# Latent attention's scores and values: the 16 meta keys as products of their own, and a new table of places for VectorE and ScalarE

## The reference

```python
s = (jnp.einsum('bqhd,bkhd->bhqk', qn, k_nope, preferred_element_type=jnp.float32)
     + jnp.einsum('bqhr,bkr->bhqk', qr, k_rope, preferred_element_type=jnp.float32)) * scale
q_idx = blk * Q_BLOCK + jnp.arange(Q_BLOCK)
mask = (key_idx[None, :] <= q_idx[:, None]) & (key_idx[None, :] >= pad)
s = jnp.where(mask[None, None], s, MASK_VALUE)
p = jax.nn.softmax(s, axis=-1)
return jnp.einsum('bhqk,bkhd->bqhd', p.astype(v.dtype), v)
```

## Time and profile before

| | |
|---|---|
| median of 3 runs | 844.8 us (844.73 to 845.4) |
| the profiled execution's own time | 846.0 us |
| span of its instructions | 844.2 us |
| PE busy | 818.6 us, 97% |
| DVE busy | 560.8 us, 66% |
| ACT busy | 532.3 us, 63% |
| granted TensorE clock, mean | 0.995 |

### The profile page before, as it was taken

One profiled execution on the slowest core, in us unless ns is written; L12 is line 12 of the kernel. 1 busy time (PEld: TensorE's weight loads), 2 busy tenths in 40 slices (PEclk: granted clock), 3 DMA queues, 4 the chain that ended last, 5 costly groups with the idle time before them and its releaser, 6 DMA issues.

```text
span 844.2 us, 16068 instructions
## 1 busy us (share of the span) xinstructions
PE 818.6 (97%) x6612; PEld 786.2 (93%) x6612; DVE 560.8 (66%) x1004; ACT 532.3 (63%) x962; POOL 2.6 (0%) x6
## 2 busy tenths in 40 slices
PE   6999999999999998899999999999999999999994
PEld 6997769999999898899999999999899999999994
DVE  6685658889988976567536553876758656465353
ACT  6478766589977868763544545668867546444442
POOL 0000000000000000000000000000000000000001
PEclk9999999999999999999999999999999999999998
DMA  8453215555745432445645764444336737374431
GB/s 313 150 188 113 63 51 172 191 162 210 231 170 170 124 124 98 155 171 166 221 163 181 250 193 150 150 151 144 107 108 217 242 119 253 113 258 167 148 101 50
DMA packets 41448, 137.39 MB, mean 163 GB/s; under 512 B 4384, under 2 KB 8736, under 8 KB 41376
## 3 DMA queue, kind: packets, MB, share of 16 engines
q1 hardware_dynamic: 41376, 136.37, 49.0%
HBM read 135.31 MB, written 1.05 MB: 162 GB/s over the span
## 4 chain that ended last, share of the span: by engine, by line
PE 94%; DVE 3%; ACT 1%; DMA 1%; issue 0%; DVEq 0%; ACTq 0%; SPq 0%
PE bank L666 26%; PE bank L668 26%; PE bank L667 25%; PE bank L671 2%; PE bank L939 2%; PE bank L672 2%; PE bank L673 2%; PE bank L891 1%; PE bank L892 1%; DVE temp L1449 1%; PE bank L860 1%; DVE residual L1449 1%; PE bank L919 1%; DMA weights_raw<-stream_dram 1%; PE bank L920 1%; DVE weights_lo L1449 1%
## 5 line engine op out<-in xcount | busy, mean ns | idle before, releaser
L666 PE MATMUL bank<-operand_hi,weights_hi 128*128 128x256 f32 (+1 forms) x1860 | 529.5, 285 | 10.9 <-DVE weights_lo L1449 7.8
L668 PE MATMUL bank<-operand_hi,weights_lo 128*128 128x256 f32 (+1 forms) x1860 | 526.7, 283 | 0.0
L667 PE MATMUL bank<-operand_lo,weights_hi 128*128 128x256 f32 (+1 forms) x1860 | 526.6, 283 | 0.0
L666 PEld LDWEIGHTS bank<-operand_hi,weights_hi 128*128 128x128 f32 x1860 | 352.4, 189 | 16.3 <-DVE weights_lo L1449 8.7
L668 PEld LDWEIGHTS bank<-operand_hi,weights_lo 128*128 128x128 f32 x1860 | 352.8, 190 | 0.0
L667 PEld LDWEIGHTS bank<-operand_lo,weights_hi 128*128 128x128 f32 x1860 | 350.8, 189 | 0.0
L1016 ACT ACTIVATE weights_hi<-weights_raw 128x1024 fp32r<-128x1024 f32 (+2 forms) x254 | 258.3, 1041 | 130.1 <-PE bank L668 92.5
L1449 DVE TENSOR_TENSOR weights_lo<-weights_raw,weights_hi 128x1024 fp32r<-128x1024 f32 (+2 forms) x254 | 298.5, 1205 | 52.5 <-ACT weights_hi L1016 52.4
L1449 DVE TENSOR_TENSOR operand_lo<-temp,operand_hi 128x512 fp32r<-128x512 f32 (+2 forms) x48 | 28.4, 601 | 55.0 <-ACT operand_hi L1016 55.0
L1455 DVE SCALAR_TENSOR_TENSOR temp<-bank,rows 128x512 f32<-128x512 f32 x32 | 21.9, 688 | 40.6 <-PE bank L668 39.7
L671 PE MATMUL bank<-weights_hi,operand_hi 128*128 128x256 f32 (+1 forms) x140 | 41.6, 297 | 0.0
(11 more groups left out here) (177 smaller groups left out, 645.3 us busy)
## 6 DMA issues: line engine op xcount, KB each, us to landing
weights_raw<-stream_dram SPq DMA_DIRECT2D x244, 512.0 KB, 4.4
weights_raw<-stream_dram SPq DMA_DIRECT2D x6, 384.0 KB, 3.5
temp<-memT_dram SPq DMA_DIRECT2D x8, 256.0 KB, 3.4
residual<-xT_dram SPq DMA_DIRECT2D x4, 272.0 KB, 4.9
weights_raw<-stream_dram SPq DMA_DIRECT2D x4, 256.0 KB, 5.1
out_dram<-residual SPq DMA_DIRECT2D x3, 256.0 KB, 2.2
constants<-consts_dram SPq DMA_DIRECT2D x1, 536.0 KB, 7.8
out_dram<-residual SPq DMA_DIRECT2D x2, 128.0 KB, 2.1
```

What stands on the lines that cost most here:

```text
L666: e.matmul(to, w_h, x_h, start=start, stop=False, skip_group_check=True)
L667: e.matmul(to, w_h, x_l, start=False, stop=False, skip_group_check=True)
L668: return e.matmul(to, w_l, x_h, start=False, stop=stop, skip_group_check=True)
```

## The change

The scores' tiles of 144 and 272 keys become a product over the keys from the 17th on (128 or 256 columns) and one over the first 16 keys, for nope and for rope. The product of the meta values' 272 columns becomes one of 256 and one of 16. The columns, and what is added to them, are the same. `start` is set only on the first product of the first two tiles. The table `TIMES` is replaced as a whole; PE's places are not.

```diff
-    ("scalar", "lambda_exp"): (25.5,),
-    ("scalar", "mla_softmax"): (23.67, 24.57, 24.86, 25.23, 25.27, 25.58, 25.69, 25.81),
+    ("scalar", "lambda_exp"): (6.25,),
+    ("scalar", "mla_softmax"): (22.88, 26.27, 26.36, 26.64, 28.67, 29.2, 29.3, 29.55),
...
                 for j, (q0, nq, nk) in enumerate(TILES_A):
-                    to = bank[b][0:nq, PROB_AT[j]:PROB_AT[j] + nk]
-                    e.matmul(to, qn[:, h, q0:q0 + nq], kn[:, h, 0:nk], start=True, stop=False, skip_group_check=True)
-                    mm = e.matmul(to, qr[half:half + ROPE, pair_, q0:q0 + nq], kr[half:half + ROPE, 0, 0:nk],
-                                  start=False, stop=True, skip_group_check=True)
+
+                    keys = [(META, nk), (0, META)] if j else [(0, META)]
+                    for qt, kt, last in ((qn[:, h, :], kn[:, h, :], False),
+                                         (qr[half:half + ROPE, pair_, :], kr[half:half + ROPE, 0, :], True)):
+                        for k0, k1 in keys:
+                            mm = e.matmul(bank[b][0:nq, PROB_AT[j] + k0:PROB_AT[j] + k1], qt[:, q0:q0 + nq], kt[:, k0:k1],
+                                          start=j < 2 and not last and k1 == keys[0][1], stop=last, skip_group_check=True)
...
-                e.matmul(o[:, 0:T1], V16[0:META, cs], pt[0:META, 0:T1], start=True, stop=False, skip_group_check=True)
+                for t0, t1 in ((META, T1), (0, META)):
+                    e.matmul(o[:, t0:t1], V16[0:META, cs], pt[0:META, t0:t1], start=t0 > 0, stop=False,
+                             skip_group_check=True)
```

More of the change, by code:

```diff
@@ L165 @@
[L165 to L179, removed]
@@ L195 @@
[L195 to L208, removed]
@@ L209 @@
[L209 to L223, removed]
@@ L224 @@
-    ("vector", "evacuate"): (7.56, 7.89, 7.33, 7.44, 10.4, 12.43, 10.8, 12.57, 12.29, 12.71, 13.33, 18.5, 22.67,
[7 rows of a table removed]
-    ("vector", "finish"): (7.67, 9.33, 0, 10.1, 28.8, 28.2, 29.33, 30.2, 30.6, 32.25, 32.5, 32.88, 68.5, 68.75,
[4 rows of a table removed]
+    ("scalar", "root"): (6.75, 13.2, 11.75, 34.2, 36.5, 75.25, 101.5, 164.67, 192.25),
+    ("scalar", "row"): (8.5, 13.4, 13.8, 34.6, 36.75, 76.38, 75.5, 102.5, 165.5, 192.5),
+    ("scalar", "latent_hi"): (13.6, 15.67, 16.67, 16.33, 18.5),
+    ("scalar", "small"): (6.5,),
@@ new lines @@
+    ("scalar", "inputs_root"): (55.5, 55.25, 60.5, 60.75),
+    ("scalar", "silu_gates"): (58.5, 61.67),
+    ("scalar", "y_b"): (60.88, 60.12, 61.33, 60.62, 64.2, 64.4, 64.6, 64.8),
+    ("scalar", "softmax"): (76.12, 76.25, 76.62, 77.33, 80.18, 80.09, 80.55, 80.45, 86.4, 86.2, 86.8, 87.33, 90.42,
+        90.75, 90.83, 90.5, 166.5, 166.75, 167.5, 168.22, 172.58, 172.08, 172.83, 172.67, 178.17, 178.33, 178.5,
+        178.58, 183.23, 183.15, 183.62, 183.46),
+    ("scalar", "softmax_scale"): (76.5, 76.75, 77.67, 77.83, 168.11, 168.33, 168.56, 168.89, 172.75, 172.5, 172.92,
+        173.33, 178.42, 178.67, 178.75, 178.83, 183.38, 183.54, 183.92, 183.77),
@@ new lines @@
+    ("scalar", "evacuate"): (9.33, 11.25, 11.5, 9.67, 10.5, 26.82, 19.5, 21.67, 15.33, 22.62, 22.12, 17.5, 20.33,
[7 rows of a table added]
+    ("vector", "total"): (0, 0, 0, 30.83, 0, 70.67, 98.67, 162.5, 189.9),
+    ("vector", "rstd"): (5.67, 12.2, 11.5, 32.2, 35.5, 72.5, 98.83, 162.75, 191.5),
+    ("vector", "rope_rows_a"): (8.38,),
+    ("vector", "latent_norm"): (12.8, 13.5, 14.38, 14.5, 17.33),
+    ("vector", "latent_rest"): (14.25, 14.75, 14.88, 17.67, 19.33),
+    ("vector", "small"): (4.5, 5.33, 17.83, 22.67, 25.5, 8.5),
@@ new lines @@
+    ("vector", "conv_rest"): (42.33, 41.4, 39.67, 42.67, 48.57, 48.43, 48.86, 48.93),
+    ("vector", "inputs"): (48.21, 48.71, 55.57, 57.25),
+    ("vector", "inputs_square"): (50.6, 50.2, 60.11, 60.39),
+    ("vector", "inputs_mult"): (55.71, 55.29, 60.56, 60.67),
+    ("vector", "scan"): (57.75, 55.86, 60.17, 55.43, 60.78, 60.89, 60.94, 61.4),
+    ("vector", "y_b"): (60.22, 57.5, 60.33, 60.44, 61.2, 61.6, 61.8, 62.33),
+    ("vector", "y_b_rest"): (60.72, 60.06, 60.83, 60.61, 62.17, 62.5, 62.67, 62.83),
@@ new lines @@
+    ("vector", "y_2"): (77.88, 79.75, 171.1, 173.4, 175.33, 178.75, 180.12, 180.62, 184.5, 186.5),
+    ("vector", "scale_x"): (77.38,),
+    ("vector", "merge"): (77.62, 79.25, 85.4, 85.8, 90.67, 90.83),
+    ("vector", "sub_mean"): (89.14, 92.33),
+    ("vector", "sub_norm"): (89.43, 92.67),
+    ("vector", "sub_turn"): (90.33, 90.5, 93.5),
+    ("vector", "evacuate"): (6.5, 6.25, 8.25, 6.75, 14.62, 8.88, 12.4, 12.6, 14.12, 17.17, 17.5, 19.67, 21.33,
[6 rows of a table added]
+    ("vector", "finish"): (8.12, 8.62, 0, 8.75, 30.5, 30.08, 30.33, 30.58, 30.75, 32.4, 32.8, 33.67, 69.4, 68.5,
[4 rows of a table added]
```

38 lines of the change are left out of this document (25 added, 13 removed), and 35 rows, old and new, of the table TIMES.

## The result

The changed kernel takes 850.3 us (848.92 to 852.23, 6 runs) against 845.3 us (844.73 to 845.76, 6 runs) before: a ratio of 1.006 with a 95% interval of 1.0046 to 1.0074, 5.0 us slower. Executions more than 1.5% above the fastest of their kernel are left out of every ratio here. A second set of runs of the same kernel, made beside the later experiments, gave 848.4 against 845.2 us: 1.0043 (1.0026 to 1.006), 3.2 us slower. The forecast was 848.8 us and slower, 847.3 to 850.3.

What follows compares the result with a forecast made beforehand. The prediction took PE's own work to bound the latent attention heads. 40 splits add +4.0 us and the table 0, so the median of 844.8 becomes 848.8 us, range 847.3 to 850.3.

Steps and rivals of the forecast that it cites:

- What bounds the kernel: Latent attention heads, 67.5 to 124 us: PE's own work sets the time; DVE and ACT have room.
- The price of a short product: 16-column products with 128-wide weights: two weight loads set 0.22 us each, about +0.10 us a split.
- The upper bound of +12 us: Split products: the long one keeps its wait, the short one shows its first load, +0.30 us a split.
- the lower of +0.9: Split products: a short one costs only 0.14 us, as with 16 wide weights, +0.02 us a split.
- about +8 us: Split products by the skill page's rule: same-row neighbours hide neither load, some 0.2 us a split.
- A change of rows, not the columns beyond 128s: Fp32 products in the heads: a changed contraction row count costs about 0.1 us behind a long product, whatever its columns.
- the rival: Heads' products: columns beyond whole 128s keep the next load waiting, so the split saves 3.0 us, 841.8; chance 0.11.
- The sum: Whole kernel: +4.0 us on PE's path from 40 splits, table 0, giving 848.8 us.
- The table: New `TIMES`: taken as 0, with -1 to +2 us, since PE's waits are the lengths of their chains.
- the -1 that I allowed: New `TIMES`: at most 1 us gained by taking away PE's waits.

Runs made afterwards that it cites:

- The double dose: The split with the table of before, each 16-column product cut again into two of 8 columns: 884.4 us, ratio 1.0453 against the kernel before.
- the order without a split: Kernel before with its table, the scores' three nope products in a row, then the three rope products: 842.5 us, ratio 0.9966.
- the split in the good order: Kernel before with its table, nope then rope products grouped, 16-column pieces split off in scores and values: 849.4 us, ratio 1.0054.
- the best one: Kernel before with grouped nope and rope products, the values' 16-row product moved last, and the new table: 839.2 us, ratio 0.9937.

## Why the prediction was right, point by point

**What bounds the kernel: right.** PE's own work set the time in the heads. What it got there (+4.1 us) moved everything behind it, and neither DVE nor ACT became late.

**The price of a short product: right.** 0.22 us was taken, from the row of the one-column products and from L983. The double dose gave 0.22 us for each added product at full clock. The upper bound of +12 us and the lower of +0.9 are out. By the sentence of the Trainium skill in "TensorE: Matmul & The Clock Gate", section "The mechanism", that a load overlaps matmuls in flight only when the row group differs, products over the same rows would hide no load, which the prediction put at about +8 us; the heads here gave +4.1. The same section also lets a load into the background weight buffer run ahead, which the prediction left out.

**A change of rows, not the columns beyond 128s: right against the rival, too narrow as a rule.** This was the step with a rival against it. Whole 128s took nothing off: with no change on either side, 144 columns take 0.247 us (the order without a split) and 128 columns 0.223 (the split in the good order), which is the price of the 16 columns and no more. But it isn't rows alone. The prediction's rule has L921 at 0.32 us because 16 rows follow; in front of scores it takes 0.32 us as well, with 128 rows and 16-wide weights behind it. The prediction had not read that row. And its 0.1 us "behind a long product" is half of the price: L920's 0.53 us, which it took as free of any change, had the 16-row product ahead of it. A product pays some 0.1 us when the change is behind it, and some 0.1 us when it is ahead. The forecast didn't suffer, since the split leaves every change where it was and only the short product takes it over.

**The sum: right for the split.** +4.0 us was taken, the heads cost 4.1 in the trace, and the split alone measured +4.4 us.

**The table: mis-sized.** I took 0, "such a wait is the length of its chain, and no order shortens it". The table alone gives -0.9 us, which is inside the -1 that I allowed. What I missed was no wait at all: I read PE's waits for what the table could take away, while 0.84 us lay in two heads' products running one behind the other with PE busy throughout, because ACT gave a bank back late. It shows in the distance from start to start of eight equal matmuls (1.98 us at 562 us, 1.14 at 558 us), which I had read for the latent attention only.

**The clock: not in the prediction.** The sum 845.3 + 4.4 - 0.9 = 848.8 is the forecast to the tenth, and the second set came out at 848.4. Some of that is luck: the forecast started 0.5 us too low, took 0.4 us too little for the split and 0.9 too much for the table, and these cancel. The first set came out at 850.3, with executions whose mean clocks, 0.988 to 0.994, all lay below the 0.995 and 0.996 of five of the other six. The prediction had the clock as the same before and after. Of all 18 executions of the split in the order of before, with either table, 7 have a mean clock of 0.993 or less, and of the kernel before 8 of 60. That leans towards the split bringing such stretches on, but 4 of the 7 come from one set, so it isn't shown. For the twice cut products (5 of 5), the good order with the split (8 of 9) and the good order alone with the table of before (9 of 12) it is plain that they come more often.

## What to carry to other kernels

Read what a product costs from the distance to the next start, and compare neighbours before columns: an odd size next to a change of contraction rows, or of the weights' width, looks dear though only the neighbour is. Order the products so that those over the same rows and with weights of the same width follow each other; that gave 0.49 us a head at full clock, where cutting off 16 columns added 0.42. A product with wide weights has a least price, 0.22 us here, whatever it moves. And look at the clock of the new order too. A list of waits shows only idle time; two pieces of work that could run side by side on PE and don't are found by comparing equal groups of instructions.

## What the hardware did that I had not expected

- **Two fp32 products on separate halves of the rows run side by side.** Eight matmuls of 256 columns, four for each of two heads with operands on 64 rows each, took 1.14 us when both heads' banks were free, and 1.98 us when the second bank came late. The latent attention's rope products use 64 rows, but each follows a nope product over all 128, so nothing there shows it.
- **A busy PE can lose its clock.** In the kernel with the short products cut once more, PE was busy for 30.40 of 30.40 us between 119.6 and 150 us at a granted clock of 0.50, level 1.2 GHz. Ahead of the fall it had done scores of mostly 8- and 16-column products, transposes and values. Of its +38.9 us the split is 4.4 and the 40 added products at 0.22 us are 8.8; some 26 us are left, and they go with the clock. The profiled execution agrees: 51 us at half clock, of which, by the scores' 6.69 against 3.76 us, 44% are lost, 22 us as an estimate, and it ran 3 us below the median.
- **Stretches of 3.4 us at half clock** appear in several kernels here, in the heads (106.6 to 110.0 us, the split in the good order), at their end (119.1 to 122.5 us) or where the second block turns its softmax (333.4 to 336.8 us in the changed kernel; 6.8 us long, from 323.3, in the best one). In the changed kernel's, 17 matmuls start where 30 did, which costs 1.5 us. How often a kernel gets one differs with its products, as counted above; which execution gets one is not explained by anything in these traces.
